# Neighbourhood attention: the reciprocal sums move from the exponentials to the table that the turns multiply with

## The reference, cut to what matters

```
s = jnp.concatenate([s_ctx, s_lat.reshape(B, H, GRID_W, kr * GRID_W)], axis=-1)
p = jax.nn.softmax(s, axis=-1).astype(vx.dtype)
...
return (jnp.einsum('bhqc,bchd->bqhd', p_ctx, vc)
        + jnp.einsum('bhqrk,brkhd->bqhd', p_lat, vb))
```

## Time and profile before

| | |
|---|---|
| median of 3 runs | 2299.44 us (2298.68 to 2300.31) |
| the profiled execution, its time | 2303.47 us |
| its span, first to last instruction | 2301.6 us |
| PE busy | 2248.9 us (98%) |
| DVE busy | 1451.6 us (63%) |
| ACT busy | 997.2 us (43%) |
| DMA, mean | 130 GB/s |

### The profile page before, as it was taken

The page is one execution under the profiler, slowest core; times in us unless marked ns, Lnnn a source line. Parts: engine busy times, 40 slices in busy tenths (PEclk is TensorE's granted clock), DMA queues, the critical chain, the costliest instruction groups (busy, mean ns, idle before and its releaser), DMA issues.

```text
span 2301.6 us, 39429 instructions
## 1 busy us (share of the span) xinstructions
PE 2248.9 (98%) x14134; PEld 1922.0 (84%) x14134; DVE 1451.6 (63%) x2070; ACT 997.2 (43%) x1454; POOL 34.6 (2%) x35
## 2 busy tenths in 40 slices
PE   8999999999999999999999999999899999999998
PEld 6788888887778888888888888788799989989998
DVE  5873577766768862777532335766664577857765
ACT  4222324544455222226422224544554457555653
POOL 0000000000000000000000000000000000000000
PEclk9999999999999999999999999999999999999999
DMA  9674555321134654554332435422255645215321
GB/s 317 208 211 119 150 174 184 118 70 60 38 92 135 204 154 114 178 165 146 104 89 85 111 92 160 131 91 92 86 153 165 187 142 156 75 38 166 101 74 56
DMA packets 403609, 298.70 MB, mean 130 GB/s; under 512 B 13454, under 2 KB 369556, under 8 KB 403348
## 3 DMA queue, kind: packets, MB, share of 16 engines
q1 hardware_dynamic: 370154, 231.59, 34.6%
q10 hardware_dynamic: 33322, 65.34, 8.7%
HBM read 295.84 MB, written 1.06 MB: 129 GB/s over the span
## 4 chain that ended last, share of the span: by engine, by line
PE 84%; DVE 7%; ACT 4%; issue 3%; DMA 1%; SPq 1%; ACTq 0%; DVEq 0%; POOL 0%; POOLq 0%
PE banks L1113 23%; PE banks L1115 23%; PE banks L1114 23%; PE banks L1403 2%; ACT wh L1909 1%; DVE wl L2618 1%; PE banks L1130 1%; PE banks L1061 1%; PE banks L1137 1%; PE banks L896 1%; PE banks L1237 1%; PE banks L967 1%; PE banks L1344 1%; PE banks L1268 1%; PE banks L1352 1%
## 5 line engine op out<-in xcount | busy, mean ns | idle before, releaser
L1113 PE MATMUL banks<-uR,wh 128*128 128x512 f32 (+2 forms) x2188 | 758.5, 347 | 9.7 <-DVEq L2457 3.9
L1114 PE MATMUL banks<-uR,wh 128*128 128x512 f32 (+2 forms) x2188 | 746.9, 341 | 0.0
L1115 PE MATMUL banks<-uR,wl 128*128 128x512 f32 (+2 forms) x2188 | 746.8, 341 | 0.0
L2618 DVE TENSOR_TENSOR wl<-wraw,wh 128x2048 fp32r<-128x2048 f32 (+2 forms) x198 | 414.7, 2095 | 323.3 <-ACTq L1838 312.5
L1909 ACT ACTIVATE wh<-wraw 128x2048 fp32r<-128x2048 f32 (+3 forms) x203 | 357.4, 1761 | 428.8 <-PE banks L1115 378.0
L1113 PEld LDWEIGHTS banks<-uR,wh 128*128 128x128 f32 (+1 forms) x2188 | 415.9, 190 | 65.9 <-issue 8.9
L1115 PEld LDWEIGHTS banks<-uR,wl 128*128 128x128 f32 (+1 forms) x2188 | 415.9, 190 | 47.3
L1114 PEld LDWEIGHTS banks<-uR,wh 128*128 128x128 f32 (+1 forms) x2188 | 416.2, 190 | 44.2
L1113 PE MATMUL banks<-gR,wh 128*128 128x512 f32 (+1 forms) x704 | 256.8, 365 | 2.1 <-DVEq L2457 2.1
L1115 PE MATMUL banks<-gR,wl 128*128 128x512 f32 (+1 forms) x704 | 255.3, 363 | 0.0
L1114 PE MATMUL banks<-gR,wh 128*128 128x512 f32 (+1 forms) x704 | 255.2, 363 | 0.0
(11 more groups left out here) (355 smaller groups left out, 2644.4 us busy)
## 6 DMA issues: line engine op xcount, KB each, us to landing
wraw<-in_ffn_w_in SPq DMA_DIRECT2D x173, 512.0 KB, 5.1
ada_buf<-in_ada_w ACTq DMA_DIRECT2D x24, 1280.0 KB, 6.0
wraw<-in_w_in SPq DMA_DIRECT2D x56, 512.0 KB, 4.7
wraw<-in_ffn_w_out SPq DMA_DIRECT2D x64, 384.0 KB, 4.0
wraw<-in_ffn_w_out SPq DMA_DIRECT2D x64, 320.0 KB, 4.5
ada_buf<-in_ada_w ACTq DMA_DIRECT2D x24, 768.0 KB, 4.6
wraw<-in_da_w_in SPq DMA_DIRECT2D x24, 512.0 KB, 4.6
wraw<-in_na_w_in SPq DMA_DIRECT2D x24, 512.0 KB, 4.5
```

The lines of the kernel that those rows point to most:

```text
L1113: mm(o, a[0], b[0], start=first, stop=False)
L1114: mm(o, a[0], b[1], start=False, stop=False)
L1115: return mm(o, a[1], b[0], start=False, stop=last)
L2618: do(V.tensor_tensor(wl[:, s, 0:n], wraw[:, s, 0:n], wh[:, s, 0:n].bitcast(F32), ALU.subtract), w_lo)
```

## The change

The exponentials stay as they are. DVE multiplies the 128 x 128 table `flip` with the reciprocal sums instead, once for each head, and writes the two scaled tables to `half`. PE multiplies the exponentials with the scaled table in an ordinary matmul (`mm` with start and stop) where it used the transpose. The operands lie as before: `prob` is the stationary one and the table the moving one. A scaled, reversed identity both turns the tile and divides each query by its sum.

```
@@ PE, na_heads
                         for kt in range(TT):
-                            ins = nc.tensor.transpose(psum[6][:, kt * P:kt * P + P], prob[:, n % 2, j, kt * P:kt * P + P], flip)
+                            ins = mm(psum[6][:, kt * P:kt * P + P], prob[:, n % 2, j, kt * P:kt * P + P],
+                                     half[:, n % 2, j * P:j * P + P], start=True, stop=True)
                         ins.then_inc(tr_full, 1)
@@ DVE, na_heads
                         do(V.reciprocal(rsum[:, b, 1, :], rsum[:, b, 0, :]))
                         for h in range(2):
-                            x = prob[:, b, h, :]
-                            do(V.tensor_scalar(x, x, rsum[:, b, 1, h:h + 1], None, ALU.mult), *([probn_ready] if h else []))
+                            do(V.tensor_scalar(half[:, b, h * P:h * P + P], flip, rsum[:, b, 1, h:h + 1], None, ALU.mult),
+                               *([probn_ready] if h else []))
```

## The result

The changed kernel takes 2309.17 us (median of 7 runs, 2305.83 to 2311.09) against 2299.44 us (7 runs). The ratio is 1.0039, with a 95% interval of 1.0029 to 1.0049: slower by 7 to 11 us, where +8.5 us was forecast.

The account below looks back on a forecast made before the run. PE, busy 98% of the span, was taken as the bound, with DVE pacing part of the tail. Steady part +8.0 us (9.9 - 1.9) and tail +0.5 us gave +8.5 us, a 2307.9 us median, range 2304.0 to 2312.0 us.

Parts of the forecast that it names:

- Two records for each matmul: In the neighbourhood attention's turns: 128 full 32-bit matmuls replace 128 transposes and show 256 records on PE.
- The price of a turn: On PE, four transposes as matmuls: 0.43 us more a turn, 9.9 us over 23 turns before the last unit.
- What the waits swallow: Steps with a projection unit: five PE waits, 2.3 us together, absorb 1.9 us of the longer turns.
- ACT's late copy: Before the product with the values: ACT's copy hangs on unit and weights, so its wait swallows up to 0.43 us.
- DVE's saving: Scalings of 128 instead of 512 columns: 6.4 us over 16 items, worth 1.2 us in the tail only.
- the steady part: Steps 0 to 22, with a projection unit in each, where PE sets the pace: +8.0 us.
- the estimate that the prediction set aside: Skill's table: 128-wide scaling takes 127 ns, tail gain some 2.2 us, whole change about 1 us cheaper.
- The tail: After the last unit: four turns cost 1.7 us more, DVE's scalings give back 1.2 us, +0.5 us in all.
- The clock: Two half-speed PE stretches between 1635.8 and 1650 us, each costing at most 1.7 us; left unchanged in the sum.
- a rival of 17%: Busier PE regains full clock at the attention's end: +6.8 or +5.1 us instead of +8.5; chance 0.17.
- The full price: Rival over all 32 turns: nothing swallowed, no DVE gain in the tail, +13.8 us, 2313.2 us; chance 0.09.
- one record for each matmul: Rival for the turns: no extra records, PE pays nothing, 2298.2 us, or 2294.8 us with the clock back; chance 0.05.

Follow-up runs that it names:

- e2: Half of the change alone against the kernel before: DVE scales the table, turns stay transposes with the unscaled table; 2297.55 us, ratio 0.9990.
- e1: Half of the change alone against the kernel before: turns as matmuls with the unscaled table, DVE still scales the exponentials; 2310.50 us, ratio 1.0042.
- e7: The kernel before, unchanged, profiled a second time; first turn to last unit 116.72 us, tail 23.30 us.
- e4: The changed kernel with the turn's two operands rounded to the reduced 32-bit format, one record a matmul; 2297.18 us, ratio 0.9989 to before.
- e12: The changed kernel with the turn's operands rounded to the reduced 32-bit format, run again to narrow the interval; 2297.69 us, ratio 0.9992 to before.
- e6: The kernel before with the change for items 0 to 11 only, the steps with a unit; ratio 1.0053.
- e10: The kernel before with the change for items 0 to 11 only, run again; ratio 1.0055.
- e9: The kernel before with the scaled table and one-pass matmuls of rounded operands for items 12 to 15 only; 2297.30 us, ratio 0.9987.
- e8: The changed kernel, unchanged, profiled a second time; first turn to last unit 125.33 us, tail 24.02 us.
- e11: The changed kernel, unchanged, profiled and timed again; 2309.25 us, ratio 1.0042 to before.
- e3: The kernel before with the four transposes of every turn issued twice, eight records a turn; 2307.93 us, ratio 1.0030.
- e5: The kernel before with the change for items 12 to 15 only, the steps without a unit; ratio 1.0011.

## Why the prediction was right, point by point

- **Two records for each matmul**: right, 256 records for 128 matmuls.
- **The price of a turn**: forecast 0.43 us (0.41 to 0.46), measured 0.47 us on average (0.44 and 0.51). The rows of the first attention gave 0.82 us for eight records, and the odd turns now take 0.80 us; the even turns, which follow the scores, take 0.92 us. The step took the price of one neighbour for both. With the unit included the price is 0.47 and 0.49 us. That is 1.1 us more over 23 turns than the 9.9 us of the sum.
- **What the waits swallow**: right in kind, too small in size: forecast 1.9 us, measured 2.4 us. 12 even turns x 0.49 + 11 odd turns x 0.47 = 11.0 us, and the landmarks show 8.61 us against the +8.0 us of the forecast. That ACT's late copy hangs on the unit and not on the turn, so that its wait is a cushion, is borne out step by step. Three odd steps, the one of 0.59 us in the earlier trace rows among them, last as long as before from the turn to the product with the values (1548.97 to 1553.03 us, now 1550.85 to 1554.90 us), so each swallows its whole turn; ACT still ends them, though the view lists no wait. Three more grow by 0.11 to 0.15 us only, and the five without a wait by 0.47 us. So six steps give way, where the view listed five waits, and the too small price of a turn was half made up by the too small cushion.
- **DVE's saving**: right in place and size. It is worth nothing in the steady part (e2: 116.74 us) and 1.2 us in the tail (e1 and e2 from both sides). A scaling takes 287 ns, not the 127 ns of the estimate that the prediction set aside.
- **The tail**: forecast +0.5 us, measured +0.72 us at full clock: four turns more on the chain at 0.48 us each (e1: 25.21 - 23.30 = 1.91 us), less 1.2 us. The chain of waits after, in order of time (start, length), has the same shape as the earlier trace rows: DVE up to the turn of item 14, then PE:

```profile
1633.86 0.30 DVE half L2898
...
1639.52 0.30 DVE half L2898
...
1640.24 1.16 PE banks L1359 x8
...
1642.13 1.17 PE banks L1359 x8
...
1645.29 1.09 PE banks L1359 x8
...
1647.11 1.17 PE banks L1359 x8
```

One detail differs: at its start the chain runs through PE and ACT (turns and copies of item 12, up to 1632.70 us) and only then joins DVE. DVE and PE are close to even there, so a further saving on DVE alone might bring less; no run tests it.

- **The clock**: the sum left it as it was, and a rival of 17% said that full speed comes back. In the tail it did, in three profiles out of three. But what a stretch costs depends on where it falls: nothing where PE waits anyway, 1.2 us in the tail, 1.5 us where PE has no waits. And the changed kernel has one behind the output projection instead. From the first turn to L1130, which holds both places, it takes 183.55, 183.13 and 183.03 us in its three profiles against 174.29 and 174.17 us: some +9.0 us, so that little or nothing was gained on balance. The sum was right to leave the clock as it was, but no row had shown why, and that was in part luck.

Steady and tail together are +9.3 us at full clock, against +8.5 us forecast and +9.7 us between the medians. The full price (13.8 us, and some 15 us at the measured 0.47 us a turn) did not come, because five of the turns fell into PE's waits in the tail, 2.4 us were swallowed in the steady part and 1.2 us came back from DVE; one record for each matmul did not come, as the earlier trace rows had shown.

## What to carry to other kernels

Ask of every saving which engine ends the stretch: 6.4 us off an engine that is hidden bought 1.2 us, and 15 us of work (32 turns x 0.47 us) given to the engine that sets the pace cost all but what its own waits and the slack of the tail took in. Count what PE has to issue, not what the code issues: a full 32-bit matmul is two records where a transpose, or a matmul of rounded operands, is one. And where two profiles differ by less than the scatter of the rest of the program, measure between landmarks around the change; here that turned a scatter of several us into one of some 0.02 us in the steady part. In the tail, look at the clock as well.

## What was not expected of the hardware

- Eight 32-bit transposes hold PE as long as four 32-bit matmuls of the same shape: 0.79 against 0.80 us after a unit.
- The same turn is dearer after the scores than after a unit: 0.92 against 0.80 us as matmuls, 0.50 against 0.40 us as one-pass matmuls, 0.41 against 0.36 us as transposes. But with the unit behind it both kinds take the same, 3.86 us as matmuls and 3.37 or 3.39 us as transposes, so a price read from two starts depends on what stands around them.
- A stretch at 1.2 GHz costs 1.5 us where PE has no waits (9.52 to 9.57 against 8.04 to 8.06 us from L1061 to L1130 in fourteen profiles), and nothing in the tail of e7.
- The slow stretches of the clock (level 1.2 GHz) are not fixed to a place in the kernel. In the eight profiles with short turns in the tail (before, e7, e2, e4, e12, e6, e10, e9) all but e10 have one in it or just after it; in five with long turns there (after, e8, e11, e1, e3) none has. e5, also with long turns, has one that begins at the output projection. The Trainium skill (TensorE: Matmul & The Clock Gate, section PE-mode transpose) says that transposes do not count as activity for the clock gate. e3, whose longer turns are all transposes, keeps the full clock in the tail in its one profile and has its slow stretches where the changed kernel has them (at 1674.4 and 1705.1 us, against 1675.3 and 1706.1 us), which does not support that rule; e10, which has the short turns and the full clock all the same, shows that one profile does not settle it.
- e6 and e10 take some 3 us more than their landmarks account for, twice. Both profiles show PE waiting for weights at the same two places outside the attention; why those weights come late there stays open.
